# The last column block one token tile at a time, the second tile in two column halves, and beta as a broadcast row

## The reference

```
def layer_norm(x, gamma, beta):
    mu = jnp.mean(xf, axis=-1, keepdims=True)
    var = jnp.mean(jnp.square(xf - mu), axis=-1, keepdims=True)
    y = (xf - mu) * lax.rsqrt(var + LN_EPS) * gamma + beta
...
    merged = g_attn * (y_attn @ w_proj_attn) + g_pool * (y_pool @ w_proj_pool)
    out = jnp.einsum('bsd,de->bse', merged, w_out)          # 256 x 2048 by 2048 x 2048
    return layer_norm(DEEPNORM_ALPHA * x + out, ln_gamma, ln_beta)
```

## Time and profile before

| | |
|---|---|
| median of 3 runs | 961.87 us (961.44 to 961.93) |
| profiled execution | 960.2 us, its span 958.4 us |
| busy PE, PEld, DVE, ACT | 947.3, 838.7, 633.7, 423.2 us |
| granted TensorE clock, mean | 0.997 |
| DMA | 177.24 MB, mean 185 GB/s |

### The profile page before, as it was taken

One profiled execution on the slowest core, in us unless ns is written; L12 is line 12 of the kernel. 1 busy time (PEld: TensorE's weight loads), 2 busy tenths in 40 slices (PEclk: granted clock), 3 DMA queues, 4 the chain that ended last, 5 costly groups with the idle time before them and its releaser, 6 DMA issues.

```text
span 958.4 us, 14944 instructions
## 1 busy us (share of the span) xinstructions
PE 947.3 (99%) x5346; PEld 838.7 (88%) x5346; DVE 633.7 (66%) x996; ACT 423.2 (44%) x592; POOL 0.2 (0%) x4
## 2 busy tenths in 40 slices
PE   8999999999999999999999999999999999999996
PEld 6998898898898898898898899888888888888884
DVE  6767567567567567567567568666666666665666
ACT  6454354354354354354354354545445444543330
POOL 0000000000000000000000000000000000000000
PEclk9999999999999999999999999999999999999998
DMA  8744454445444445544444445655555554555532
GB/s 320 283 176 176 176 176 176 175 175 175 175 175 175 176 174 175 175 175 175 177 173 175 176 174 219 221 178 210 182 178 197 186 183 177 213 204 196 182 126 88
DMA packets 27543, 177.24 MB, mean 185 GB/s; under 512 B 3455, under 2 KB 4223, under 8 KB 7039
## 3 DMA queue, kind: packets, MB, share of 16 engines
q1 hardware_dynamic: 26928, 173.53, 50.1%
q10 hardware_dynamic: 596, 3.45, 1.0%
HBM read 174.87 MB, written 2.10 MB: 185 GB/s over the span
## 4 chain that ended last, share of the span: by engine, by line
PE 96%; DVE 1%; DMA 1%; SPq 1%; issue 0%; ACT 0%; DVEq 0%
PE proj_ps L337 40%; PE proj_ps L338 20%; PE attn_ps L337 6%; PE attn_ps L331 4%; PE attn_ps L332 4%; PE attn_ps L333 4%; PE attn_ps L338 3%; PE value_ps L332 3%; PE value_ps L333 3%; PE value_ps L331 3%; PE mixed_ps L445 1%; DMA w_raw<-in_weights 1%; PE mixed_ps L331 1%; PE mixed_ps L333 1%; PE mixed_ps L332 1%; PE attn_ps L406 1%
## 5 line engine op out<-in xcount | busy, mean ns | idle before, releaser
L337 PE MATMUL proj_ps<-xt,w_hi 128*128 128x512 f32 x1664 | 586.9, 397 | 1.8 <-DVE w_lo L756 1.0
L338 PE MATMUL proj_ps<-xt,w_lo 128*128 128x256 f32 x1664 | 466.9, 281 | 0.0
L727 DVE TENSOR_TENSOR w_lo<-w_raw,w_hi 128x1024 fp32r<-128x1024 f32 x318 | 374.2, 1220 | 81.5 <-ACT w_hi L576 80.1
L337 PEld LDWEIGHTS proj_ps<-xt,w_hi 128*128 128x128 f32 x1664 | 312.9, 188 | 76.3 <-DVE xt L749 1.5
L576 ACT ACTIVATE w_hi<-w_raw 128x1024 fp32r<-128x1024 f32 x318 | 318.3, 1051 | 54.1 <-PE mixed_ps L333 27.1
L338 PEld LDWEIGHTS proj_ps<-xt,w_lo 128*128 128x128 f32 x1664 | 315.0, 189 | 0.0
L595 ACT ACTIVATE corr<-proj_ps 128x256 f32<-128x256 f32 x104 | 39.9, 384 | 288.0 <-PE proj_ps L338 288.0
L741 DVE TENSOR_TENSOR qk_f<-proj_ps,corr 128x256 f32<-128x256 f32 x48 | 20.3, 424 | 79.0 <-ACT corr L595 79.0
L337 PE MATMUL attn_ps<-yp,w_hi 128*128 128x512 f32 x128 | 45.9, 397 | 0.0
L337 PE MATMUL attn_ps<-ya,w_hi 128*128 128x512 f32 x128 | 45.6, 396 | 0.0
L331 PE MATMUL attn_ps<-w_hi,xt 128*128 128x384 f32 x128 | 42.9, 335 | 0.0
(11 more groups left out here) (151 smaller groups left out, 884.4 us busy)
## 6 DMA issues: line engine op xcount, KB each, us to landing
w_raw<-in_weights SPq DMA_DIRECT2D x158, 1024.0 KB, 4.8
res<-in_x_rows ACTq DMA_DIRECT2D x1, 2048.0 KB
out_rows<-res SPq DMA_DIRECT2D x8, 256.0 KB, 2.2
xt_raw<-in_xt SPq DMA_DIRECT2D x3, 512.0 KB, 6.7
w_raw<-in_weights SPq DMA_DIRECT2D x6, 256.0 KB, 6.5
w_raw<-in_weights SPq DMA_DIRECT2D x2, 512.0 KB, 9.2
gamma<-in_gamma_row ACTq DMA_DIRECT2D x1, 1024.0 KB
mask<-in_mask SPq DMA_DIRECT2D x1, 576.0 KB, 4.4
```

What stands on the lines that cost most here:

```text
L337: mm(bank, w_hi[:, slot, cols], tile.rearrange("p a s -> p (a s)"), start=first, stop=False)
L338: return mm(bank[:, SEQ:2 * SEQ], w_lo[:, slot, cols], tile[:, 0, :], start=False, stop=last)
L727: tt(w_lo[:, slot, cols], w_raw[:, slot, cols], w_hi[:, slot, cols].bitcast(F32), ALU.subtract).then_inc(lo_split, 1)
```

## The change

Stage C's last block (chunks 157 to 160) is done in another order. PE first does all sixteen k tiles for token tile 0, through all four chunks. Then it does tile 1 in two column halves of 256 (`last_sum`), each through all four chunks again. For that all four chunks must be in SBUF at once: the fourth goes to `last_hi` and `last_lo`, placed where `xt` lay, and its split no longer waits for a free slot. `chunk_done` is not signalled for these chunks; `first_rows_done` and the new `last_rows_done` are.

`beta` comes as a row repeated on 128 partitions (1 MB, one more DMA on ACT's queue). With it DVE computes shift * gamma + beta itself (`normalise_here`) for all four column blocks of tile 0 and for the first of tile 1. PE's way over `turn` and a matmul is left for blocks 1 to 3 of tile 1 only. The split of the five rows moves to behind block 0 (`split_rows`). Tile 1's last block is added, measured and scaled in halves (`last_half`), so that its statistics have five groups.

```diff
+        _, (last_hi, last_lo, beta, shifted) = place(base, [...])
+        def last_sum(h):
+            return attn_ps[:, 3 * 512:3 * 512 + HALF_BLOCK] if h == 0 else mixed_ps[:, 0:HALF_BLOCK]
...
-            for n in range(C_FIRST, CHUNKS - 1):
+            for n in range(C_FIRST, CHUNKS - BLOCK_CHUNKS):
...
-            pe.wait_ge(lo_split, 2 * CHUNKS)
-            for t in range(TT):
-                for kk in range(BLOCK_KT):
-                    done = out_products(CHUNKS - 1, kk, t)
-                done.then_inc((first_rows_done, chunk_done)[t], 1)
...
+            for n in range(CHUNKS - BLOCK_CHUNKS, CHUNKS):
+                for kk in range(BLOCK_KT):
+                    if kk % 2 == 0:
+                        pe.wait_ge(lo_split, 2 * n + kk // 2 + 1)
+                    done = out_products(n, kk, 0)
+            done.then_inc(first_rows_done, 1)
+            for h in range(2):
+                pe.wait_ge(rows_added, (TT + 2, TT * 3)[h])
+                for k in range(KT):
+                    n, kk = CHUNKS - BLOCK_CHUNKS + k // BLOCK_KT, k % BLOCK_KT
+                    cols = slice(kk * BLOCK + h * HALF_BLOCK, kk * BLOCK + (h + 1) * HALF_BLOCK)
+                    done = product(last_sum(h), merged[:, k, 0, P:SEQ], merged[:, k, 1, P:SEQ],
+                                   out_weights(n, 0)[:, cols], out_weights(n, 1)[:, cols], k == 0, k == KT - 1)
+                done.then_inc(last_rows_done, 1)
...
-            turn_row(0)
-            for c in range(BLOCKS):
-                shift_product(0, c)
-            turn_row(1)
-            for c in range(BLOCKS):
-                shift_product(1, c)
+            turn(value_ps[0:ROWS, 0:P], shift_parts[:, 1, 0:ROWS], ident[:, :]).then_inc(row_turned, 1)
+            for c in range(1, BLOCKS):
+                mm(norm_shift(c)[:, :], shift_rows[0:ROWS, 1, :], row_parts[0:ROWS, c * BLOCK:(c + 1) * BLOCK],
+                   start=True, stop=True).then_inc(norm_shift_ready, 1)
...
             act.dma_start(gamma[:, :], gamma_d).then_inc(tail_landed, 16)
+            act.dma_start(beta[:, :], beta_d).then_inc(tail_landed, 16)
...
+            def last_half(h):
+                dve.wait_ge(last_rows_done, h + 1)
+                stt(out=at, in0=at, scalar=ALPHA, in1=last_sum(h), op0=ALU.mult, op1=ALU.add).then_inc(rows_added, 1)
+                chain.add(nc.vector.bn_stats(stats[:, 1, BLOCKS - 1 + h, :], at))
+                if h == 1:
+                    variance(1)
+                chain.add(tt(at, at, gamma[:, cols], ALU.mult))
...
+            def normalise_here(t, c):
+                chain.link(stt(out=shifted[:, c % 2, :], in0=gamma[:, cols], scalar=shift[:, t:t + 1],
+                               in1=beta[:, cols], op0=ALU.mult, op1=ALU.add))
+                stt(out=at, in0=at, scalar=rstd[:, 2 + t:3 + t], in1=shifted[:, c % 2, :],
+                    op0=ALU.mult, op1=ALU.add).then_inc(out_ready, 1)
...
+                    if c == 0:
+                        split_rows()
...
-            token_shift(0)
-            token_shift_lo(0)
-            add_rows(c, 1)
-            statistics(c, 1)
-            variance(1)
-            normalise_rows(0, 0)
-            token_rstd(1)
-            times_gamma(c, 1)
-            token_shift(1)
-            token_shift_lo(1)
-            for b in range(1, BLOCKS):
-                normalise_rows(0, b)
-            for b in range(BLOCKS):
-                normalise_rows(1, b)
+            token_shift(0, False)
+            for b in range(BLOCKS):
+                normalise_here(0, b)
+            last_half(0)
+            last_half(1)
+            token_rstd(1)
+            token_shift(1, True)
+            normalise_here(1, 0)
+            for b in range(1, BLOCKS):
+                normalise_rows(1, b)
```

More of the change, by code:

```diff
@@ L172, in layer_kernel @@
             ("shift_rows", [TT, P], F32R), ("row_parts", [D_MODEL], F32R)])
+        _, (last_hi, last_lo, beta, shifted) = place(base, [
+            ("last_hi", [CHUNK], F32R), ("last_lo", [CHUNK], F32R), ("beta", [D_MODEL], F32),
+            ("shifted", [2, BLOCK], F32)])
         _, (corr_pair, pair_f) = place(at_szp, [("corr_pair", [2, SEQ], F32), ("pair_f", [2, SEQ], F32)])
@@ L508, in _, with out_weights @@
                     next_bank(B_FIRST, j, i)
+            def out_weights(n, part):
+                return (last_hi, last_lo)[part][:, :] if n == CHUNKS - 1 else (w_hi, w_lo)[part][:, n % RING, :]
             def out_products(n, kk, t):
@@ L687, in _ @@
                     split_hi(C_FIRST, j + AHEAD, i, RING)
-            for e in range(whole * RING + AHEAD, OT):
+            for e in range(whole * RING + AHEAD, OT - 1):
                 split_hi(C_FIRST, e, 0, 0)
+            landed(act, CHUNKS - 1, 0, 0, 0)
+            for half in range(2):
+                cols = slice(half * HALF * P, (half + 1) * HALF * P)
+                activation(last_hi[:, cols], w_raw[:, (CHUNKS - 1) % RING, cols], ACT.Copy).then_inc(hi_split, 1)
             activation(rstd[:, 4:5], ident[:, 0:1], ACT.Sqrt)
@@ L695, in _ @@
                 activation(rstd[:, t:t + 1], mv[:, t, 2:3], ACT.Sqrt).then_inc(std_ready, 1)
[L696 to L698 removed]
+            act.wait_ge(row_turned, 1)
+            activation(shift_rows[0:ROWS, 1, :], value_ps[0:ROWS, 0:P], ACT.Copy).then_inc(shift_rows_ready, 1)
         @block.vector
@@ L969, in normalise_rows, with split_rows @@
             def normalise_rows(t, c):
-                dve.wait_ge(norm_shift_ready, t * BLOCKS + c + 1)
+                dve.wait_ge(norm_shift_ready, c)
                 at = res[:, t, c * BLOCK:(c + 1) * BLOCK]
-                stt(out=at, in0=at, scalar=rstd[:, 2 + t:3 + t], in1=norm_shift(t, c)[:, :],
+                stt(out=at, in0=at, scalar=rstd[:, 2 + t:3 + t], in1=norm_shift(c)[:, :],
                     op0=ALU.mult, op1=ALU.add).then_inc(out_ready, 1)
+            def split_rows():
+                chain.link(copy(rows_hi[0:ROWS, :].bitcast(F32R), rows[0:ROWS, :]))
+                chain.link(ts(rows_signed[0:ROWS, :], rows_hi[0:ROWS, :], row_kind[0:ROWS, 1:2], None, ALU.mult))
+                stt(out=row_parts[0:ROWS, :], in0=rows[0:ROWS, :], scalar=row_kind[0:ROWS, 0:1],
+                    in1=rows_signed[0:ROWS, :], op0=ALU.mult, op1=ALU.add).then_inc(rows_split, 1)
@@ L976, in _ @@
             chain.link(nc.vector.memset(shift_parts[:, :, :], 1.0))
             for e in range(OT - 1):
-                if e + AHEAD < OT:
+                if e + AHEAD < OT - 1:
                     split_lo(C_FIRST, e + AHEAD, 0, 0)
+                if e + AHEAD == OT - 1:
+                    for half in range(2):
+                        cols = slice(half * HALF * P, (half + 1) * HALF * P)
+                        dve.wait_ge(hi_split, 2 * (CHUNKS - 1) + half + 1)
+                        tt(last_lo[:, cols], w_raw[:, (CHUNKS - 1) % RING, cols], last_hi[:, cols].bitcast(F32),
+                           ALU.subtract).then_inc(lo_split, 1)
@@ L992, in _ @@
                         times_gamma(c, t)
-            chain.link(copy(rows_hi[0:ROWS, :].bitcast(F32R), rows[0:ROWS, :]))
-            chain.link(ts(rows_signed[0:ROWS, :], rows_hi[0:ROWS, :], row_kind[0:ROWS, 1:2], None, ALU.mult))
-            stt(out=row_parts[0:ROWS, :], in0=rows[0:ROWS, :], scalar=row_kind[0:ROWS, 0:1],
-                in1=rows_signed[0:ROWS, :], op0=ALU.mult, op1=ALU.add).then_inc(rows_split, 1)
+                    if c == 0:
+                        split_rows()
             c = BLOCKS - 1
```

48 lines of the change are left out of this document (21 added, 27 removed).

## The result

The changed kernel takes 955.0 us (median of 6 runs, 954.13 to 955.43) against 961.65 (6 runs, 960.37 to 962.4) beside it: a ratio of 0.9932 [0.9921, 0.9944]. The forecast was 959.4 with a range of 958.5 to 960.9. The profiled execution took 954.86.

What follows compares the result with a forecast made beforehand. PE was taken to bound the kernel until its last sum, then DVE in the tail; 0.07 (earlier sum), 1.34 and 1.06 us less made 2.47, so 961.87 - 2.5 = 959.4 us, range 958.5 to 960.9.

Steps and rivals of the forecast that it cites:

- What bounds the kernel now: Whole kernel: PE bounds until its end, then DVE; the change works on the 8.35 us between 947.41 and 955.76.
- PE's end: Last block: 256-column steps of 0.1183 us, last matmul starting at 947.03, DVE beginning at 947.34 against 947.41.
- Sum: Whole kernel: span 958.4 less 2.47 is 955.93; measured time 961.87 less 2.5 is 959.4 us.
- rival 5: Tail: more gain than forecast, full clock and faster output drain together, 958.0 to 958.8 us; chance 0.08.
- Rival 3: Last block's 256-column steps: weight loads bind at 0.188 us each, 6.7 us more, 966.1 us in all; chance 0.06.
- From the sum to the last shift part: Tail, from tile 1's last sum being ready: 2.24 us instead of 3.58, 1.34 less.
- From there to the end: Tail, from the last shift part to DVE's end: 3.71 us instead of 4.77, 1.06 less.
- were it full, 0.14 more gain: Tail's first product: half clock was kept at 0.77 us; at full clock DVE's own 951.09 binds, 0.14 us more gain.
- The halves: Tile 1's last block: 256-wide operations lose 0.16 us each on DVE, but gain 0.26 on each of two behind PE's end.
- Splits in time: Tile 0's pass: DVE splits chunks 159 and 160 before PE wants them, smallest margin 0.5 us, no stall.
- Under cover: Block 0: the moved `split_rows`, 4.90 us, and beta's DMA, 3.2 us of transfer, hide behind PE at no cost.
- can't begin before 896.6 anyway: Chunk 154: its delayed load goes out at 891.0, lands by 895.8, and its rounding starts no earlier than 896.6 regardless.

Runs made afterwards that it cites:

- e1: The kernel before with only the statistics tile `stats` made twice as large, moving tiles behind it by 192 bytes; 957.39 us, ratio 0.9964.
- e3: The changed kernel with the wide `stats` put where `xt` lay, all other tiles at their old addresses; 958.52 us, 0.9975 of the kernel before.
- e5: The changed kernel with the 256-column matmul first in odd k tiles of stages A and B; 955.33 us, 0.9943 of the kernel before.
- e8: The changed kernel with `ya` and all tiles behind it on a multiple of 128 bytes; 955.73 us, 0.9948 of the kernel before.
- e12: The changed kernel with each tile group at the address modulo 256 where its stage ran fastest; 949.4 us, 0.9872 of the kernel before.
- e0: The kernel before, unchanged, run and traced again; 961.14 us, ratio 1.000.
- e6: The changed kernel with tile 1's last sum in one 512-column piece instead of column halves; 955.52 us, 0.9946 of the kernel before.
- e9: The kernel before with `ya` and all tiles behind it moved by 256 bytes; 960.86 us, run once.
- e13: The kernel before with only `merged` (and `yp_f` behind it) moved by 32 bytes to a multiple of 128; 959.0 us, one execution.
- e15: The kernel before with only `ya` moved by 192 bytes, the tiles behind it by 256; 961.08 us, one execution.
- e7: The kernel before with a 192-byte gap ahead of the attention phase's tiles, `yp` and `merged` only; 957.77 us, ratio 0.9973.
- e4: The kernel before with the last group's two value tiles multiplied in the other order in each head's mixing step; 960.92 us, ratio 1.0001.
- e2: The kernel before with only the beta input, its 1 MB DMA and one more semaphore added, none used; 961.19 us, ratio 1.0001.
- e11: The kernel before with `ya` and all tiles behind it moved by 128 bytes; 957.64 us, run once.
- e10: The kernel before with `ya` and all tiles behind it moved by 64 bytes; 959.88 us, run once.
- e14: The kernel before with DVE's and ACT's work tiles moved by 192 bytes, attention tiles, `yp` and `merged` by 256; 960.62 us, one execution.

## Why the prediction was right and wrong

**The step that failed** is in "What bounds the kernel now" and "PE's end": the prediction lets the change work only on the 8.35 us behind 947.41, keeps the last block's first matmul at 924.59, and so "Sum" takes "Span 958.4 - 2.47". The stretch ahead of 924.59 was put at no change without a reason; the wide `stats`, which moves the tiles behind it by 192 bytes, was never priced. That stretch was worth -5.50 + 1.60 = -3.9 us (e1: 3.65 by medians, e3 without it: none). None of the five rivals named it; rival 5, "full clock and faster drain together" (958.0 to 958.8), was the only one on this side, and had another mechanism and the wrong size. The chain was 96% PE, and PE's step was taken as a constant.

**The tail's sum was right, in part by luck.** Forecast 2.47 less, measured 2.50 by the traces and 0.9975 of 961.04, or 2.5, by e3. DVE ends 28.70 us after the last block's first matmul, just as forecast (953.29 - 924.59), but the terms missed and cancelled: 0.17 more, 0.04 and 0.13 less. By terms, with times from that matmul:

- PE's end. The 256-column steps took (944.37 - 932.97) / 95 = 0.120, not 0.1183, and DVE began at 22.92 instead of 22.75: 0.17 lost. Rival 3 (loads bind, 0.188) was wrong.
- From the sum to the last shift part: 946.89 - 944.69 = 2.20 against 2.24.
- From there to the end: 950.47 - 946.89 = 3.58 against 3.71. The first product is 0.46 long, not 0.77, and the window around it shows 0.88 granted clock; the half-clock stretch comes behind it. So the branch "were it full, 0.14 more gain" came true, by chance. The same code in e5, e8 and e12, after the same idle time of 2.45 us before the turn, had its first product at half clock for all or part of it (0.76, 0.76 and 0.64 long); e3's was at full clock (0.47). With half clock the way to the end took 951.13 - 947.33 = 3.80 in e5, and DVE ended at 28.90: 0.2 us of the profiled gain is luck of that execution. Before and e0, one and the same kernel, differ in this too: the second turn (L544) is 0.27 long in the one and 0.38 in the other. The Trainium skill ("TensorE: Matmul & The Clock Gate", Part 1) says that idleness brings the throttled clock back: it did in each of these kernels, at 0.50 granted, but at another point of the tail from one to the next.
- The halves. By DVE's rows, a gain of 0.26 on each of two operations. e6 against e5, both at half clock, shows 0.75 saved behind PE's end (sum, statistics and the gamma step) and 0.31 given back by later readiness. The Trainium skill's rule against small tiles ("Advanced Engine Details and Errata", The Read-Write Bubble) holds for an engine's total, two 0.42 against one 0.69, and decides nothing where half of it is hidden: the end comes 0.44 us later with whole tiles.

One reading of the prediction was off and changed nothing: all eight L973 stand behind tile 1's statistics, and seven behind its last shift part, the number that the sum used.

**Splits in time: right.** The last two splits run from 925.70 and 927.97, 3.93 and 6.20 after the block's start; tile 0's pass has 11.20 busy of 11.20 us. The forecast had the second of them at 930.87 - 924.59 = 6.28.

**Under cover: right.** `split_rows` moved to behind block 0 and PE idled nowhere. Rows of DVE, its first operation and the weight splits behind it:

```profile
880.90 1.21 DVE L1006 CAST rows_hi<-rows 5x2048 fp32r<-5x2048 f32 x1
...
885.73 6.88 DVE L738 TENSOR_TENSOR w_lo<-w_raw,w_hi 128x1024 fp32r<-128x1024 f32 x6
```

Six splits follow without a gap: DVE works off the delay. ACT did wait for the load that this delayed, that of chunk 154. It came in 6.4 us after the split that freed its slot (888.0 to 894.42), not the 4.8 forecast:

```profile
894.42 2.01 ACT L583 ACTIVATE w_hi<-w_raw 128x1024 fp32r<-128x1024 f32 x2 [4.04 <-DMA w_raw<-in_weights]
```

Its rounding starts 921.77 - 894.42 = 27.35 us ahead of the last block; in before it waited for PE alone and was 0.45 earlier, at 924.59 - 896.79 = 27.80:

```profile
896.79 2.01 ACT L576 ACTIVATE w_hi<-w_raw 128x1024 fp32r<-128x1024 f32 x2 [3.59 <-PE attn_ps L333]
```

So the forecast that it "can't begin before 896.6 anyway" was 0.45 short, and harmless. Beta's DMA raised the DMA share of the matching stretch from 0.77 to 1.02, 291 to 432 GB/s, with PE busy 5.60 of 5.60 us. DVE stood idle 1.57 us before it could take tile 1's last sum, against 1.2 forecast.

**What stays open.** Shown is that the places of the tiles alone, taken modulo 256, set the stages' lengths (e1, e3, e9), and which stage hangs on which: C on `merged` (e13) and part of B on `ya` (e15), both operands of PE, and A on the tiles of the attention phase as a group (e7). That in stage A too it is PE's own reads is argued, not shown. Nor is it shown how. The matmuls of stage A that slow down read `xt` and the weight slots, which never moved; most likely they take their cadence from neighbours that read the moved tiles. Stage B agrees: its chunks on `xt` take 177.7 us in before and 180.5 in e7, where `yp` and `merged` moved and `xt` didn't. That neighbours carry it is still an inference: e4 tried to break it by another order and could not. Why 96 is slow for the attention tiles and 128 fast for `merged` isn't explained by any run.

## What to carry to other kernels

Where one engine is nearly the whole chain, 96% here, price each line of a diff that moves an address, not only those that move work: a tile grown by 192 bytes was worth more than the whole rewritten tail. Compare the stages' lengths, start to start, before explaining a result by the part that was edited; two kernels that should agree there to 0.01 us and don't have another cause. And put such a tile at the end of the list, or try a few offsets of the big operands: here that gave 5.6 us more (955.0 to 949.4; 5.0 by the stages' lengths) for no instruction at all. And where a tail hangs on the clock, compare two kernels only at the same clock: 0.2 of the 0.64 us between e6 and after came from it.

## What the runs showed that I had not expected

- PE's step depends on where tiles lie modulo 256 bytes, at full granted clock and with no wait: 512 columns at 0.2333 or 0.2267 us (stage C), a k tile of 512 + 256 columns at 0.353 or 0.347, seven heads of stage A at 503.01 to 497.51 us, B at 271.36 to 266.65.
- PE kept either cadence on the same operands. Over 112 matmuls of head 0, which read only `xt` and weights, before takes 19.43 us:

```profile
24.93 0.39 PE L337 MATMUL proj_ps<-xt,w_hi 128*128 128x512 f32 x1
...
44.36 0.33 PE L333 MATMUL attn_ps<-w_hi,xt 128*128 128x384 f32 x1
```

and e2, with all of PE's operands at the same addresses, 19.77:

```profile
26.13 0.40 PE L340 MATMUL proj_ps<-xt,w_hi 128*128 128x512 f32 x1
...
45.90 0.33 PE L336 MATMUL attn_ps<-w_hi,xt 128*128 128x384 f32 x1
```

The profiled executions of after, e0, e8, e11, e12 and e13 took 19.41 to 19.43 here, those of e1, e3, e4, e6, e7, e9, e10, e14 and e15 19.76 to 19.80 (e5, with its other order, 19.53). In head 0 the placement of the moved tiles doesn't decide it (before and e9 differ); from head 1 on it does. The kernel before was profiled twice (before, e0) and was fast here both times, the others once, so whether one kernel can show both, and whether that is a part of the spread between its runs (960.27 to 962.15 in 26 runs of before), is open.
- The half clock began at another point of the same tail from kernel to kernel: before the first product of e8 and e5, within that of e12, behind it in after and e3. The prediction rightly priced both cases; they differ by 0.2 us.
